# Router on the residual rows among the output products, two more pairs' second weights beside them, and the first tile's rows built by PE from token hits

## The reference

```python
x = x + mixer(h, ...)                    # ends in merged @ w_out
h = rms_norm(x, g_ffn)
g_logits = ht @ w_gr + b_gr              # 4 groups
grp = argmax(g_logits)
e_logits = ht @ w_er + b_er              # 8 experts of each group; the group's own are kept
top_vals, top_idx = top_k(e_logits, 2)
p_in = softmax(top_vals) * p_grp
# each chosen expert: silu(h @ w_gate) * (h @ w_up) @ w_down, weighted by p_in, summed
return rms_norm(x + moe, g_final)
```

## Time and profile before

| | us |
|---|---|
| median of 3 runs | 670.78 |
| lowest, highest | 668.95, 678.31 |
| the profiled execution | 679.34 |
| its span, first to last instruction | 677.5 |
| PE busy in it | 573.9 |
| DVE, ACT, POOL busy | 342.7, 257.6, 296.1 |

### The profile page before, as it was taken

The page is one execution under the profiler, slowest core; times in us unless marked ns, Lnnn a source line. Parts: engine busy times, 40 slices in busy tenths (PEclk is TensorE's granted clock), DMA queues, the critical chain, the costliest instruction groups (busy, mean ns, idle before and its releaser), DMA issues.

```text
span 677.5 us, 12329 instructions
## 1 busy us (share of the span) xinstructions
PE 573.9 (85%) x4305; PEld 385.9 (57%) x4308; DVE 342.7 (51%) x847; ACT 257.6 (38%) x445; POOL 296.1 (44%) x470
## 2 busy tenths in 40 slices
PE   3899999999999999999998308799989859696882
PEld 2577788876665777777888204444445424243430
DVE  4418999999988993478131581211211201111145
ACT  6444433246565746533224003334333323232222
POOL 5434434479996213355810026445445442525221
PEclk9999999999999998999997557999999989999997
DMA  9222724232202033034068986999899999999863
GB/s 296 64 69 63 249 62 119 68 91 74 71 15 63 1 124 125 1 125 155 1 249 282 412 319 222 406 409 408 312 403 409 408 409 408 408 402 399 326 260 124
DMA packets 59118, 149.23 MB, mean 220 GB/s; under 512 B 8836, under 2 KB 25220, under 8 KB 59086
## 3 DMA queue, kind: packets, MB, share of 16 engines
q1 hardware_dynamic: 53582, 139.89, 55.5%
q0 software_dynamic: 5360, 8.41, 3.5%
q10 hardware_dynamic: 144, 0.52, 0.2%
HBM read 145.37 MB, written 12.60 MB: 233 GB/s over the span
## 4 chain that ended last, share of the span: by engine, by line
PE 53%; DVE 21%; SPq 11%; DMA 6%; issue 4%; ACT 3%; POOL 1%; DVEq 0%; POOLq 0%; ACTq 0%
PE bank L689 26%; PE bank L958 10%; SPq L416 8%; PE bank L975 5%; DVE bm L1386 4%; DVE m L1385 4%; DVE conv_buf L1377 3%; DMA gates<-in_w_e_up 3%; PE bank L767 2%; SPq L426 2%; PE bank L902 2%; PE bank L931 2%; DMA region<-expert_rows 2%; PE bank L800 1%; PE bank L788 1%
## 5 line engine op out<-in xcount | busy, mean ns | idle before, releaser
L689 PE MATMUL bank<-h_hi,w_part 128*128 128x512 f32 (+1 forms) x528 | 173.4, 398 | 3.2 <-DVE h_lo L1335 1.7
L538 POOL TENSOR_TENSOR w_part<-region,w_part 128x1024 fp32r<-128x1024 f32 (+1 forms) x52 | 109.9, 2114 | 147.5 <-ACT w_part L1040 147.5
L689 PEld LDWEIGHTS bank<-h_hi,w_part 128*128 128x128 f32 (+1 forms) x528 | 98.0, 186 | 30.4 <-issue 6.8
L958 PE MATMUL bank<-region,kT 128*32 128x256 f32 x1536 | 93.7, 398 | 16.2 <-DMA region<-in_w_e_up 12.0
L1702 DVE TENSOR_TENSOR mask_b<-mask_b,bank 128x128 f32<-128x128 f32 x30 | 8.7, 288 | 188.3 <-ACT mask_b L1288 113.1
L689 PE MATMUL bank<-h_lo,w_part 128*128 128x512 f32 (+1 forms) x264 | 103.0, 390 | 0.0
L958 PEld LDWEIGHTS bank<-region,kT 128*32 128x32 f32 x1536 | 56.1, 115 | 61.0 <-issue 37.3
L1040 ACT ACTIVATE w_part<-region 128x1024 fp32r<-128x1024 f32 (+1 forms) x52 | 48.0, 925 | 108.1 <-PE bank L689 107.9
L588 POOL TENSOR_TENSOR carrier<-mhalf 128x1 f32<-128x1 f32 x185 | 34.0, 201 | 123.8 <-ACT qT L1295 108.6
L1420 DVE SCALAR_TENSOR_TENSOR bank<-glu,cv,bank 128x256 f32<-128x256 f32 x196 | 78.6, 479 | 0.0
L975 PE MATMUL bank<-region,mask_b 128*32 128x512 f32 x384 | 46.2, 598 | 11.3 <-DVE mask_b L1705 11.3
(11 more groups left out here) (273 smaller groups left out, 882.5 us busy)
## 6 DMA issues: line engine op xcount, KB each, us to landing
region<-in_w_e_down SPq DMA_DIRECT2D x22, 1024.0 KB
region<-in_w_e_gate SPq DMA_DIRECT2D x44, 512.0 KB
region<-in_w_e_up SPq DMA_DIRECT2D x44, 512.0 KB
region<-in_w_in SPq DMA_DIRECT2D x16, 1024.0 KB, 6.1
gates<-in_w_e_gate SPq DMA_DIRECT2D x20, 512.0 KB
gates<-in_w_e_up SPq DMA_DIRECT2D x20, 512.0 KB
conv_buf<-in_w_e_down SPq DMA_DIRECT2D x10, 1024.0 KB
region<-in_w_out SPq DMA_DIRECT2D x2, 2048.0 KB, 7.9
```

The source lines that it names most:

```text
L538: g.tensor_tensor(unit_part(u, 1), unit_raw(u), unit_part(u, 0).bitcast(F32), ALU.subtract)\
L689: last = mm(out_, a_parts[p], b_parts[q], start=start and x_ == 0, stop=stop and x_ == 2)
L958: last = mm(bank[0][32 * c:32 * c + 32, 0:FF], xTs[:, k, at_:at_ + 32], w_gu[slot][:, e, :, half, k, j * P:(j + 1) * P], start=(half == 0 ...
```

## The change

Three things are changed, and some that follow from them.

1. The router works on the residual rows x instead of h2: the column factor g_ffn is multiplied into the router weights (by DVE, with `gffn_T`), and the row factor rstd into the logits. PE transposes a row's half (`transpose_x2`, 4 transposes) as soon as its residual is added, in turns `x2_turns`, and forms the logits of a half (`router_logits`), between the output products. ACT moves seven of the eight turns, DVE the last. The router weights are now loaded by rows (k p), behind p = 9.
2. The second weights of pairs 1 and 2 are issued behind the first loads of slot 0, ahead of the wait for the output products. Slot 2's first weights wait for the first tile's rows on PE (`xg_mm`).
3. The rows of tile 0 are not gathered. DVE forms `first_hit` (128 tokens by 2 experts by 32 places) from the ranks of the first pair, and PE multiplies h2 rows by it, 32 products, straight into the banks that the transposes of a tile would fill. POOL gathers tiles 1, 2, 3, 4. Tiles' copies to `xg` start at tile 1, behind the column work.

The transposes of the placement matrix move behind the last tile, `place` behind the last rows on ACT, and the final sums are put in another order. Some scratch tiles move.

```diff
+        first_hit = kTf[:, BANK:BANK + 2 * TB * SLOTS].rearrange("p (b e n) -> p b e n", b=TB, e=2)
+        x2_turns = [(0, 0), (1, 0), (0, 1), (2, 0), (3, 0), (1, 1), (2, 1), (3, 1)]
@@ SP
-                    sp.dma_start(wr_g[:], w_gr[0].rearrange("(p k) g -> p k g", k=KD)).then_inc(ld_router, 16)
-                    sp.dma_start(wr_e[:], w_er[0].rearrange("g (p k) e -> p g (k e)", k=KD)).then_inc(ld_router, 16)
+                if p == 9:
...
+                        sp.dma_start(wr_g[:], w_gr[0].rearrange("(k p) g -> p k g", k=KD)).then_inc(ld_router, 16)
+                        for gr in range(NG):
+                            sp.dma_start(wr_e[:, gr, :, :], w_er[0, gr].rearrange("(k p) e -> p k e", k=KD))\
+                                .then_inc(ld_router, 16)
+                        sp.dma_start(gffn_T[:], g_ffn.rearrange("a (k p) -> p (a k)", k=KD)).then_inc(ld_router, 16)
...
+            sp.wait_ge(S["unit_mm"], WO1)
+            load_down(1, pair_at(1))
+            load_down(2, pair_at(2))
             sp.wait_ge(S["wo_mm"], TB)
...
-            load_down(1, pair_at(1))
 
             sp.wait_ge(st_h2, 16 * TB)
-            sp.wait_ge(S["x2_mm"], 2 * TB)
+            sp.wait_ge(S["xg_mm"], 2)
             for half in range(2):
                 load_half(2, pair_at(2), half)
-            sp.wait_ge(S["rt_mm"], 1)
-            load_down(2, pair_at(2))
@@ POOL
-            gather(0, 0)
             gather(1, 1)
-            pool.wait_ge(gathered[0], 16)
-            hold(2, S["rows_ready"])
             gather(2, 2)
-            gather(3, 3)
             pool.wait_ge(gathered[1], 16)
             hold(3, S["rows_ready"])
-            pool.wait_ge(S["xg_ready"], 1)
+            gather(3, 3)
             gather(RING, 0)
@@ PE
+            def transpose_x2(b, hf):
+
+                turn = x2_turns.index((b, hf))
+                pe.wait_ge(S["wo_ev"], TB * hf + b + 1)
+                if turn >= 2:
+                    pe.wait_ge(S["x2_ev"], turn - 1)
...
+            merged_rest(3, rest[3:4])
+            router_logits(3, 0)
+            transpose_x2(3, 1)
+            router_logits(3, 1)
...
+            pe.wait_ge(S["xg_ready"], 1)
+            pe.wait_ge(S["h2_ready"], TB)
+            pe.wait_ge(S["x2_ev"], 2 * TB)
+            for k in range(KD // 2):
+                for half in range(2):
+                    for b in range(TB):
...
+                        last = mm(to[:, half, :, :], rows[:, k, :], first_hit[:, b, :, :],
+                                  start=(b == 0), stop=(b == TB - 1))
@@ ACT
+            act.wait_ge(S["xg_mm"], 2)
+            a(xTs[:, 2:4, :].rearrange("p k n -> p (k n)"), bank[7][:, 0:2 * P], ACT.Copy).then_inc(S["xtev_v"], 1)
+            act.wait_ge(S["col_ready"], 1)
             for b in range(TB - 1):
                 last = a(diag[:, b, :], ident[:], ACT.Copy, scale=wts[:, 1, b:b + 1])
@@ DVE
+                if b == TB - 1:
+                    dve.wait_ge(S["x2_mm"], 2 * TB)
+                    v.tensor_copy(x2_T(2 * TB - 1), bank[7][:]).then_inc(S["x2_ev"], 1)
                 mean_square(1, b)
...
+            for b in range(TB):
+                last = v.scalar_tensor_tensor(lg[:, b, :], bank[1][:, b * LW:(b + 1) * LW], rs[:, 1, b:b + 1], br[:],
+                                              ALU.mult, ALU.add)
...
+            link(v.scalar_tensor_tensor(hic[:].rearrange("p (b e) -> p b e", b=TB), ranks[:, :, e0:e0 + 2], 1.0,
+                                        Mb[:, :, e0:e0 + 2], ALU.add, ALU.mult))
+            v.tensor_tensor(first_hit.rearrange("p b e n -> p (b e) n"), spread(iota[:, 1:SLOTS + 1], 1, 2 * TB),
+                            spread(hic[:], 2, SLOTS), ALU.is_equal).then_inc(S["xg_ready"], 1)
```

More of the change, by code:

```diff
@@ L889, in _, with merged_rest @@
             pe.wait_ge(S["branch_ev"], 2 * KD)
-            for b in range(TB):
-                for u in range(WO1, NUNIT):
+            def merged_rest(b, units):
+                for u in units:
                     if b == 0:
@@ L895, in _ @@
                         last = merged_products(1, b, u, kk)
-                last.then_inc(S["wo_mm"], 1)
-            def router_logits(b):
-                pe.wait_ge(S["x2_ev"], 2 * b + 2)
-                for k in range(KD):
-                    last = mm(bank[1][:, b * LW:(b + 1) * LW], h2T[:, k, b * P:(b + 1) * P], wr[:, k, :],
+                if u == NUNIT - 1:
+                    last.then_inc(S["wo_mm"], 1)
+            def transpose_x2(b, hf):
[3 more added lines that the diff above has]
+                    pe.wait_ge(S["x2_ev"], turn - 1)
+                for kk in range(4):
+                    k = 4 * hf + kk
+                    last = tr(bank[6 + turn % 2][:, kk * P:(kk + 1) * P], xr[:, b, k * P:(k + 1) * P], ident[:])
+                last.then_inc(S["x2_mm"], 1)
@@ L903, in router_logits @@
+            def router_logits(b, hf):
+                turn = x2_turns.index((b, hf))
+                pe.wait_ge(S["x2_ev"], turn + 1)
+                for k in range(4 * hf, 4 * hf + 4):
+                    last = mm(bank[1][:, b * LW:(b + 1) * LW], x2_T(turn)[:, (k - 4 * hf) * P:(k - 4 * hf + 1) * P], wr[:, k, :],
                               start=(k == 0), stop=(k == KD - 1))
-                if b == TB - 1:
+                if (b, hf) == (TB - 1, 1):
                     last.then_inc(S["rt_mm"], 1)
+            rest = range(WO1, NUNIT)
@@ L933, in transpose_tile @@
                         last.then_inc(S["xg_mm"], 1)
-            pe.wait_ge(S["col_ready"], 1)
-            for b in range(TB):
-                last = tr(bank[5][:, b * P:(b + 1) * P], col_w[:, b, :], ident[:])
-            last.then_inc(S["place_mm"], 1)
-            pe.wait_ge(S["x2_ev"], 2 * TB)
-            transpose_tile(0)
             def pair_tiles(n, slot, turn):
@@ L1253, in _, with x2_square, x2_out @@
                 split_hi(u)
[L1255 removed]
+            def x2_square(b):
                 act.wait_ge(S["wo_ev"], TB + b + 1)
[L1257 removed]
+                a(h2row[:, b, :], xr[:, b, :], ACT.Square,
                   accum_out=ss[:, 1, b:b + 1]).then_inc(S["ss_done"], 1)
[L1259 to L1264 removed]
+                act.wait_ge(S["ss_done"], TB + b + 1)
+            def x2_out(turn):
+                act.wait_ge(S["x2_mm"], turn + 1)
+                a(x2_T(turn), bank[6 + turn % 2][:], ACT.Copy).then_inc(S["x2_ev"], 1)
+            x2_out(0)
+            x2_out(1)
+            x2_square(0)
+            x2_out(2)
+            x2_out(3)
+            x2_square(1)
+            x2_out(4)
+            x2_out(5)
+            x2_square(2)
+            x2_out(6)
+            x2_square(3)
             act.wait_ge(S["exp_in"], 1)
@@ L1303, in _ @@
                 last.then_inc(S["yev_a"], 1)
+            act.wait_ge(S["place_mm"], 1)
+            a(place, bank[5][:], ACT.Copy).then_inc(S["place_ev"], 1)
             for b in range(TB):
@@ L1733, in _ @@
             hidden(early + 1)
-            for b in range(3):
+            for b in range(2):
                 add_row(b, 0)
@@ L1741, in _ @@
             add_row(3, 1)
[L1742 to L1746 removed]
             mean_square(2, 1)
             scale_out(1, whole)
[L1749 removed]
+            for k in range(4, 8):
                 add_late(k)
```

103 lines of the change are left out of this document (61 added, 42 removed).

## The result

| | before | after |
|---|---|---|
| median of 20 executions each | 678.10 us (668.95 to 681.81) | 669.77 us (667.74 to 672.47) |
| ratio of the fast executions, 95% interval | | 0.9908 (0.9887 to 0.9929) |
| profiled execution, its span | 679.34, 677.5 us | 668.14, 666.4 us |
| granted clock, mean over the span | 0.942 | 0.951 |

The two medians lie 8.3 us apart (1.2%). The ratio in the table leaves out before's slowest executions and is 0.9% under 1, so the gain is sure of its sign but well under 2%. The forecast was 655.3 us (650 to 663). The time lies 14.5 us above it and outside the range, for two reasons of about the same size: the gain was 8 and not 15.5, and the median of before, 670.78 from three executions, is 678.10 from twenty.

A forecast was written before the change was run, and what follows sets the result against it. No engine alone was taken to bound the kernel: PE's tiles and the weight stream must both start earlier. Tiles 15.5, held to 15 by the stream, plus 1.0 tail, less 0.5 clock: 15.5 off 670.78, 655.3 us (650 to 663).

The forecast's parts named there:

- the router's 6,144 pieces: Router weight loads between window loads p=9 and p=10: small pieces take 8 us, hidden with 4 us to spare.
- The tail's 1.0: After the last tile: late sums follow the second row add instead of the third, gaining 1.0 us, between 0 and 2.
- load 128x128 weights as the logits did, at 0.10 each at full and 0.20 at half clock: PE's 32 products for tile 0's rows: 0.22 us each taken with 64 columns, 7 us, off the path.
- Logits among the output products: 24 logit products on PE between output products at full clock: 2.5 us of the 6.4 by which these end later.
- Token products: PE's 32 products for tile 0's rows: 7 us, 377 to 384, inside DVE's 12 us on ranks and tables.
- the slow clock: Rival: tile 0's second products and tile 1 at 1.2 GHz lose 1.9 and 2.7; gain 11, 660 us; chance 0.16.
- Forecast for the tiles 15.5: Tile 0's second products at 401.4 instead of 416.94, tile 1 at 403.6 instead of 419.09: 15.5 us earlier.
- PE's entry into the loop, 0.90: Between the token products' end at 389.0 and tile 0's first products at 390.0: 0.90 us for PE to enter.
- the rival on the stream's rests: Rival: the weight stream keeps more rests; gain 12.5 if the dip shrinks nothing, 657.5 us; chance 0.08.
- the four logit reads: DVE reads the logits in four instructions where one took 0.31: between 0.3 and 1.2 us, 0.5 taken.
- DVE's two added instructions: Right after the rank products, for tile 0 from hits: between 0.5 and 0.8 us, 0.6 taken.
- POOL's slack ahead of tile 2's hold: POOL's gather for tile 2: hold near 406, ahead of use at about 407.5, only 1.5 us of slack.

The follow-up runs named there:

- the kernel with even loads: Changed kernel with DVE storing h2 rows in order (k q), so PE's weights for tile 0's rows lie side by side; median 669.25 us, ratio to before 0.9899.
- The split kernel: Changed kernel with three quarters of the token products ahead of the table, the last behind it, and diagonals moved to the last two tiles; 670.57 us, 0.9905 to before.
- the kernel with constant products ahead: Changed kernel with 32 products of constants on PE between the last logits and the wait for the ranks; median 670.26 us, ratio to before 0.9887.

## Why the prediction was wrong, point by point

**The mechanism was right.** The output products grew, most of the router's work moved in among them, the first tile no longer waits for the gather, the rest at 404 to 414 is gone, the router's 6,144 pieces are hidden (the split of the earlier trace rows starts at 138.33, in before at 138.49), and tile 0's first products came 12.3 earlier by the mark (393.03 and 408.64). The tail's 1.0 is not shown: from the last tile's first products to the end, before's two profiles take 34.6 and 36.0 us and after's three 33.4 to 34.2, a difference of 0.4 to 2.6.

**Step that failed: "load 128x128 weights as the logits did, at 0.10 each at full and 0.20 at half clock"**. The earlier trace rows shows 12 records in 1.24 us, and I took a record for a product. A float32 product is two records (the 32 logit products of before stand as x64, the 32 token products as x64), while a transpose is one. Both sums on it are short by about a factor of two:
- Logits among the output products: 5.1 us from start to start (5.8 of PE's busy time), not 2.5. 24 products are 48 records. The last residual starts at 363.39 in after and 358.15 in before, the first 3.3 earlier, so the output products grew by 8.6 and not 6.4: 5.1 for the logits, 2.8 for the 28 transposes (forecast 3.6), and 0.1 for each of the seven times that the 128x512 products start again (forecast 0.3 in all). The logits are done 2.3 later by the mark than forecast.
- Token products: 15.20 us, not 7, with 1.3 of it from the distance of their columns (13.91 in the kernel with even loads). The prediction had the bound in it: over 11 us they would delay the table, us for us. The table was due at 384.9 by the mark and came at 390.63, 5.7 late; 2.3 of that are the logits', 3.5 the token products'. Halving them gave back 3.5 at the table.

**Rival that came true: the slow clock.** Between 397 and 403 PE was busy for 2.1 of 6 us, at a clock of 1.00, and then the clock fell until 410 (us; PE busy, count; clock; DMA share, GB/s):

```profile
403.00:410.00 7.00, 6.09 (x41) 0.52 1.03 403
397.00:403.00 6.00, 2.10 (x32) 1.00 1.03 404
```

The rival had 4.6 us for it; it cost 2.8 in the two groups of products (3.64 for 1.92, 4.78 for 3.66), 2.2 of them on the way to the third tile. The Trainium skill ("TensorE: Matmul & The Clock Gate", HAM oscillation) has the slow clock come back after idle gaps between bursts, and the trace agrees: PE was idle for 3.8 us ahead of 402.18, and the clock is 0.50 from 404 on. The split kernel, whose second products came 4.9 earlier, had them in 1.92.

**The sum, mended.** Forecast for the tiles 15.5. Off it 2.3 (logits), 3.5 (token products ahead of the table), 2.2 (clock), and 0.6 between the table and tile 0's second products: 6.9 are left. That last 0.6 is the column work, 9.8 from the table's start where before had 9.4, and the way from silu to second products, 1.6 for 1.45. The first products started 0.6 later than forecast too, but were done at 398.35, ahead of the column work at 400.46, so they are off the path; and what the prediction took for PE's entry into the loop, 0.90, is in the earlier trace rows a wait for DVE's copy. The third tile's gain by the mark is 7.1 (90.3 and 83.2). S has 0.7 more, 7.8, which arise behind the third tile and are not traced to the tail; that the two sums meet so closely is in part luck, since two profiles of one kernel differ by up to 1.8 in S. The stream gave no more than the tiles did: its load for slot 2 stood behind the late token products, and the products of the earlier trace rows, which wait for weights, moved from 592.34 to 581.83, 3.3 by the mark and 7.2 by the change.

**The base.** The forecast put the gain under the median of three executions, 670.78, though the profiled one had taken 679.34. Twenty gave 678.10. 7.3 us of the miss of 14.5 are this and no step of the argument; with its gain of 15.5 the forecast would have stood at 662.6, and the other 7.2 are above all the failed step and the slow clock. The 657.5 us of the rival on the stream's rests do not follow from its gain of 12.5, which makes 658.3 on that base.

**Right and not tested by itself:** the four logit reads (0.73, forecast 0.5), DVE's two added instructions (0.17 and 0.43, forecast 0.6), POOL's slack ahead of tile 2's hold (its copy starts at 407.88, and PE needs it only behind tile 1's first products).

## What to carry to other kernels

Count the records of a product before pricing it: take a row of the same type and shape whose products you can count in the code, and divide by these. Work moved into another engine's gap is paid twice if a load waits for it as well; loosen that wait (here by loading the half of the area that isn't in use) before shortening the chain, since either alone may bring nothing, as here. And take the base from more than three executions when the profiled one is over 1% off their median.

## What was new on the hardware

- Float32 products with 128x128 weights: two loads and two products each in the trace. 128 columns side by side load in 0.19 us at full clock, and a record of 36 columns comes every 0.11 to 0.12; at half clock they load in 0.33, and a record of 64 columns comes every 0.22 (even loads, 13.91 us for 64). 128 columns 16 bytes apart load in 0.31 to 0.33 at either clock, and a record of 64 columns comes every 0.24.
- PE lost its full clock while it was busy without a pause: in the stretch of before at 267.5 us, with PE busy from 260 on; in the kernel with 24 logit products more at 362.8, busy from 355 on; and in the kernel with constant products ahead from 382 us on, inside token products that kept it busy for 4.00 of 4 us. So idle gaps are not the only thing ahead of a fall. What is needed to keep the clock the runs don't show.
- 4.2 MB of loads that were moved under the output products cost these nothing that can be seen: from the first residual to the last it took 30.27 us at 278 GB/s, and 30.28 at 139 GB/s in the kernel that loads them late.
